# MoE ends by TensorE: first pair's rows picked, and last four experts' rows spread, by matrix products

## The reference, cut to what matters

```
t = rms_norm(h) (512 x 1024)
group = argmax of 4 group logits; p_group = its softmax value
the two best of the 8 experts in that group, weights softmax(top values) * p_group
y[token] = sum over its 2 experts of weight * (silu(t w1[e]) * (t w3[e])) w2[e]
h = h + y
```

## Time and profile before

| | us |
|---|---|
| median of 3 runs | 1840.77 (1838.44 to 1843.23) |
| the profiled execution | 1835.3 |
| its span, first to last instruction | 1833.6 |
| PE busy in it | 1609.1 |

### The profile page before, as it was taken

How to read it: one execution, slowest core, us unless ns; L and a number is a source line. 1 busy time by engine, 2 the same in 40 slices (tenths; PEclk the granted TensorE clock), 3 DMA queues, 4 the chain that set the end, 5 groups by cost and what they waited for, 6 DMA issues and landing times.

```text
span 1833.6 us, 26659 instructions
## 1 busy us (share of the span) xinstructions
PE 1609.1 (88%) x11565; PEld 840.2 (46%) x11565; DVE 600.6 (33%) x1162; ACT 416.6 (23%) x823; POOL 168.6 (9%) x189
## 2 busy tenths in 40 slices
PE   4999989998899999969878589999999997988871
PEld 2444468887454454534323244445544545333330
DVE  5210766663561121434111131206410324421114
ACT  2103245553300221301000120007511303010001
POOL 2000122330000000011111200000000000111102
PEclk9999999999899999979989879999999997998996
DMA  6119000000541411369999542211015024799994
GB/s 231 46 46 315 0 3 4 4 4 3 206 163 67 184 46 55 120 249 414 423 425 423 231 185 92 92 46 47 1 54 221 0 96 194 304 423 425 425 410 168
DMA packets 82071, 313.87 MB, mean 171 GB/s; under 512 B 18088, under 2 KB 19168, under 8 KB 57184
## 3 DMA queue, kind: packets, MB, share of 16 engines
q1 hardware_dynamic: 69280, 282.76, 39.3%
q0 software_dynamic: 11520, 25.19, 3.7%
q10 hardware_dynamic: 1152, 4.19, 0.6%
HBM read 305.81 MB, written 35.39 MB: 186 GB/s over the span
## 4 chain that ended last, share of the span: by engine, by line
PE 71%; issue 7%; DVE 5%; ACT 3%; DMA 2%; POOL 1%; PEld 0%; DVEq 0%; SPq 0%; POOLq 0%; ACTq 0%
PE PS L2097 14%; PE PS L545 14%; PE PS L559 11%; PE PS L1013 7%; PE PS L2122 6%; PE PS L1351 5%; PE PS L1337 2%; PE PS L2082 2%; PE PS L1313 1%; PE PS L1548 1%; PE PS L1569 1%; PE PS L484 1%; PE PS L1559 1%; PE PS L1701 1%; PE PS L1146 1%
## 5 line engine op out<-in xcount | busy, mean ns | idle before, releaser
L545 PE MATMUL PS<-arena,ring 128*128 128x512 f32 (+1 forms) x1024 | 414.9, 567 | 0.0
L545 PEld LDWEIGHTS PS<-arena,ring 128*128 128x128 f32 x1024 | 195.0, 191 | 216.4 <-issue 211.1
L559 PE MATMUL PS<-ring,arena 128*128 128x512 f32 x448 | 194.0, 592 | 0.7 <-ACT arena L1514 0.7
L2097 PE MATMUL PS<-ring,arena 128*64 128x512 f32 x512 | 131.6, 673 | 49.8 <-issue 46.8
L2097 PE MATMUL PS<-arena 128*64 128x512 f32 x512 | 121.8, 631 | 16.4 <-issue 13.6
L559 PEld LDWEIGHTS PS<-ring,arena 128*128 128x128 f32 x448 | 84.6, 190 | 104.3 <-issue 103.3
L1351 PE MATMUL PS<-ring,arena 128*128 128x512 f32 x256 | 113.6, 595 | 0.0
L2097 PEld LDWEIGHTS PS<-ring,arena 128*64 128x64 f32 x512 | 44.0, 155 | 135.5 <-issue 132.1
L2105 DVE TENSOR_TENSOR arena<-PS,arena 128x256 f32<-128x256 f32 x32 | 13.6, 425 | 273.8 <-PE PS L2112 253.4
L573 ACT ACTIVATE arena<-PS 128x512 f32<-128x512 f32 (+1 forms) x56 | 31.7, 566 | 307.4 <-PE PS L545 307.4
L2102 ACT ACTIVATE arena<-PS 128x256 f32<-128x256 f32 x32 | 12.3, 384 | 366.1 <-PE PS L2097 366.1
(11 more groups left out here) (295 smaller groups left out, 1923.8 us busy)
## 6 DMA issues: line engine op xcount, KB each, us to landing
arena<-in_moe_w SPq DMA_DIRECT2D x96, 1024.0 KB, 8.2
ring<-in_moe_w SPq DMA_DIRECT2D x96, 1024.0 KB
ring<-in_sb_wqkv SPq DMA_DIRECT2D x6, 2048.0 KB, 8.1
ring<-in_xa_wkv SPq DMA_DIRECT2D x4, 2048.0 KB, 15.6
ring<-in_xa_wq SPq DMA_DIRECT2D x4, 2048.0 KB, 8.5
ring<-in_xa_wo SPq DMA_DIRECT2D x4, 2048.0 KB, 13.7
h<-in_x SPq DMA_DIRECT2D x8, 512.0 KB, 5.2
ring<-in_rw_wr SPq DMA_DIRECT2D x2, 2048.0 KB, 13.2
```

Source lines behind the costliest of these rows:

```text
L545: ins = pe.matmul(PS[:, g % NBANK, 0:n], ring[:, u % RING, k, P * (j % 4):P * (j % 4) + P], xt[:, k, 0:n], start=(k == 0), stop=(k == KC - 1))
L559: ins = pe.matmul(PS[:, g % NBANK, :], xt[:, k, P * t:P * t + P], ring[:, (u0 + half) % RING, k, :], start=(k == 0), stop=(k == KC - 1))
L2097: ins = pe.matmul(bank(2, 2, F)[r, :, :], xgT[p][:, k, r], w[a][:, :, k, :], start=(k == 0), stop=(k == KC - 1))
```

## The change

It has three parts, in both layers.

1. The rows of the first pair are no longer gathered. `place` adds, for each tile, four DVE operations that make a matrix `first_of` (128 tokens x 128 slots) with 1/rms where a token stands in a slot of pair 0. In `moe_route_pe`, PE multiplies h by it (`first_rows`, 8 products of 128 x 128 x 128 for each of the 4 tiles, summed in banks 0 and 1), which gives the rows already turned. `first_rows(0)` stands ahead of `route_ranks(3)`, and `first_rows(1)` and `(2)` stand ahead of the last `filled_table`. POOL fetches from pair 1 on.
2. The outputs of pairs 14 and 15 (four experts) are no longer stored. They stay in the two buffers `ye`. While pairs 5 and 9 run, DVE makes their gate matrices (`spread_vec`, 12 operations each), PE turns them at pairs 7 and 11 (`spread_pe`, 4 transpositions each), DVE copies them out at 8 and 12 (`spread_out`). At the end PE multiplies them with `ye` (`combine_last_pe`, 4 tiles x 2 halves x 2 pairs = 16 products of 128 x 128 x 512), and DVE adds the result from PSUM to h (`combine_last_vec`, 8 additions of 128 x 512). ACT copies out both halves of pair 15.
3. The gathers of `moe_combine_pool` wait for the stores of pairs 0 to 13 alone and no longer for `over_done`; their additions (`combine_stored`) stand behind DVE's last copy of the pipeline. SP's loads for layer 1 no longer wait for the gathers. In `sb_proj_pe`, the turn of tile t waits for tile t + 1 too.

The weights are split over `w_stored`, `w_last` and `w_over` by 8 further small DVE operations in `over_slots` and `over_rows`. The block for experts with over 64 tokens uses other buffers and adds its rows by itself; that part of the diff, and lines of counts and addresses, are left out here.

```diff
@@ -1445,7 +1445,7 @@
 
         def sb_proj_pe(pe):
             for t in range(NT):
-                late_turn(pe, "mix1", t, lambda e, t: e.wait_ge(S("h_moe0"), t + 1))
+                late_turn(pe, "mix1", t, lambda e, t: e.wait_ge(S("h_moe0"), min(t + 2, NT)))
             project_T(pe, FIRST["sq"], UNITS.index("sqkv"), xTS, T, lambda e, k: late_there(e, "mix1", k))
             pe.wait_ge(S("mix1_diag"), NT)
             for t in range(NT):
...
@@ -1720,16 +1727,29 @@
 
         def moe_route_pe(pe, l):
             def filled_table(t):
-                pe.wait_ge(S("onehots"), 28 * l + 3 * (t + 1))
+                pe.wait_ge(S("onehots"), 32 * l + (5, 9, 12, 15)[t])
                 for k in range(2):
                     ins = pe.matmul(PS[:, 5, 0:NPE], OS[:, t, k, :], OB[:, t, k, :], start=(t + k == 0),
                                     stop=(t + k == NT))
                 return ins
 
+            def first_rows(t):
+                pe.wait_ge(S("onehots"), 32 * l + (5, 9, 12, 16)[t])
+                for k in range(KC):
+                    ins = pe.matmul(bank(k // 4, 4, P)[:, k % 4, :], h[:, t, k::KC], first_of[:, t, :],
+                                    start=(t == 0 and k % 4 == 0), stop=(t == NT - 1 and k % 4 == 3))
+                return ins
+
             for t in range(NT - 1):
                 filled_table(t)
+            first_rows(0)
             route_ranks(pe, l, NT - 1)
+            first_rows(1)
+            first_rows(2)
             filled_table(NT - 1).then_inc(S("tabled"), 1)
+            for p in range(2):
+                pe.nop().then_inc(S(f"xg_free{p}"), 1)
+            first_rows(NT - 1).then_inc(S("xg_free0"), 1)
             pe.wait_ge(S("chosen"), 2 * NT * (l + 1))
             scores_read(pe, l, 8)
             pe.matmul(PS[:, 4, 384:384 + NE], ones[:, :], cum[:, NT, :], start=True, stop=True).then_inc(S("ranked"), 1)
...
@@ -1846,6 +1866,15 @@
                     vec.tensor_scalar(OS[:, t, k, :], iob, s8[:, m:m + 1], tokid[:, t:t + 1], ALU.is_equal, ALU.mult)\
                         .then_inc(S("onehots"), 1)
 
+                w = first_w[:, :]
+                do(vec.tensor_scalar(w, OB[:, t, :, 0], rstd[:, t:t + 1], None, ALU.mult))
+                for k in range(2):
+                    m = NT * k + t
+                    ins = vec.tensor_scalar(first_k[:, k, :], iob, s8[:, m:m + 1], w[:, k:k + 1], ALU.is_equal, ALU.mult)
+                do(ins)
+                vec.tensor_tensor(first_of[:, t, :], first_k[:, 0, :], first_k[:, 1, :], ALU.add)\
+                    .then_inc(S("onehots"), 1)
+
             for t in range(NT):
                 add(0, t)
             vec.wait_ge(S("iota_ready"), 12)
...
@@ -1965,6 +1996,13 @@
             do(vec.tensor_tensor(den, den, gsum, ALU.mult))
             do(vec.reciprocal(wA, den))
             do(vec.tensor_tensor(wB, wA, ed, ALU.mult))
+            w8 = masks[:, 3, 28:36]
+            do(vec.tensor_tensor(w_over, w8, g8, ALU.mult))
+            do(vec.tensor_tensor(w_stored, w8, w_over, ALU.subtract))
+            do(vec.tensor_tensor(w_last[1], w_stored, is_15, ALU.mult))
+            do(vec.tensor_tensor(is_late, w_stored, is_late, ALU.mult))
+            do(vec.tensor_tensor(w_last[0], is_late, w_last[1], ALU.subtract))
+            do(vec.tensor_tensor(w_stored, w_stored, is_late, ALU.subtract))
             vec.wait_ge(S("tabled"), 9 * l + 9)
             vec.tensor_scalar(table[:, NPE:NCOL], PS[:, 5, NPE:NCOL], float(NO_ROW), None, ALU.add)\
                 .then_inc(S("over_known"), 1)
@@ -2041,11 +2079,11 @@
             pool.wait_ge(S("xg_cleared"), 2 * l + 2)
             pool.wait_ge(S("rows_out"), 16 * NT * (l + 1))
             pool.wait_ge(S("table_ready"), l + 1)
-            for n in range(4):
+            for n in range(1, 4):
                 fetch(n)
             pool.wait_ge(S("out_rows_known"), l + 1)
             pool.wait_ge(S("spare_filled"), 16 * (NE * BLK // T + 2))
-            for n in range(NPE):
+            for n in range(NPE - 2):
                 if n + 4 < NPE:
                     fetch(n + 4)
                 pool.wait_ge(S("ye_a"), NPE * l + n + l + 2)
@@ -2058,24 +2096,67 @@
         def moe_combine_pool(pool, l):
             pool.wait_ge(S("pos_known"), l + 1)
             for p in range(2):
-                pool.wait_ge(S(f"ye_out{p}"), 16 * (NPE // 2) * (l + 1))
-            pool.wait_ge(S("over_done"), l + 1)
+                pool.wait_ge(S(f"ye_out{p}"), 16 * stored(p) * (l + 1))
             for t in range(NT):
                 for k in range(2):
                     pool.indirect_dma_start(out=yg[2 * t + k], out_offset=None, in_=scratch["blocks"],
                                             in_offset=bass.IndirectOffsetOnAxis(ap=pos[:, t, k:k + 1], axis=0))\
                         .then_inc(S(f"yg_in{t}"), 16)
 
-        def moe_combine_vec(vec, l):
+        def combine_stored(vec, l, t):
+
+
+            vec.wait_ge(S(f"yg_in{t}"), 32 * (l + 1))
+            for k in range(2):
+                m = NT * k + t
+                vec.scalar_tensor_tensor(out=h[:, t, :], in0=yg[2 * t + k], scalar=w_stored[:, m:m + 1], in1=h[:, t, :],
+                                         op0=ALU.mult, op1=ALU.add).then_inc(S("h_stored"), 1)
+                vec.wait_ge(S("h_stored"), 8 * l + 2 * t + k + 1)
+
+        def last_bank(t, half):
+
+            return (4 + 2 * t + half) % 8
+
+        def combine_last_pe(pe, l):
+            pe.wait_ge(S("gates_last"), 10 * l + 6)
+            pe.wait_ge(S("ye_a"), (NPE + 1) * (l + 1))
+            pe.wait_ge(S("ye_v"), (NPE + 1) * (l + 1))
             for t in range(NT):
-                vec.wait_ge(S(f"yg_in{t}"), 32 * (l + 1))
-                for k, w in enumerate((wA, wB)):
-                    if k:
-                        vec.wait_ge(S("h_half"), NT * l + t + 1)
-                    vec.scalar_tensor_tensor(out=h[:, t, :], in0=yg[2 * t + k], scalar=w[:, t:t + 1], in1=h[:, t, :],
-                                             op0=ALU.mult, op1=ALU.add)\
-                        .then_inc(S("h_half") if k == 0 else S(f"h_moe{l}"), 1)
-
+                for half in range(2):
+                    for p in range(2):
+                        ins = pe.matmul(PS[:, last_bank(t, half), :], gatesT[p][:, t, :],
+                                        ye[p][:, 512 * half:512 * half + 512], start=(p == 0), stop=(p == 1))
+                ins.then_inc(S("gates_last"), 1)
+
+        def combine_last_vec(vec, l):
+            for t in range(NT):
+                vec.wait_ge(S("gates_last"), 10 * l + 7 + t)
+                for half in range(2):
+                    v = h[:, t, 512 * half:512 * half + 512]
+                    ins = vec.tensor_tensor(v, v, PS[:, last_bank(t, half), :], ALU.add)
+                ins.then_inc(S(f"h_moe{l}"), 1)
+
+        def spread_vec(vec, l, p):
+
+
+            do = stepper(vec, l)
+            for t in range(NT):
+                for k in range(2):
+                    m = NT * k + t
+                    do(vec.tensor_scalar(gates_k[:, k, :], iob, s8[:, m:m + 1], w_last[p][:, m:m + 1], ALU.is_equal,
+                                         ALU.mult))
+                do(vec.tensor_tensor(gates_n[:, t, :], gates_k[:, 0, :], gates_k[:, 1, :], ALU.add))
+            vec.nop().then_inc(S("gates_last"), 1)
+
+        def spread_pe(pe, l, p):
+            pe.wait_ge(S("gates_last"), 10 * l + 3 * p + 1)
+            for t in range(NT):
+                ins = pe.transpose(PS[:, 3, P * t:P * t + P], gates_n[:, t, :], ident[:, :])
+            ins.then_inc(S("gates_last"), 1)
+
+        def spread_out(vec, l, p):
+            vec.wait_ge(S("gates_last"), 10 * l + 3 * p + 2)
+            vec.tensor_copy(gatesT[p].rearrange("p t s -> p (t s)"), PS[:, 3, :]).then_inc(S("gates_last"), 1)
 
         def turn_rows(pe, p, rows):
             for k in range(KC):
...
@@ -2162,14 +2248,12 @@
                 pe.wait_ge(S("ye_v"), NPE * l + n + l + 1)
                 down(pe, p, 2, 1).then_inc(S("down_done"), 1)
 
-            pe.wait_ge(S("table_ready"), l + 1)
-            for p in range(2):
-                pe.nop().then_inc(S(f"xg_free{p}"), 1)
-            turn(0)
             for n in range(NPE):
                 up_pair(n)
                 if n == 4:
                     over_table_pe(pe, l)
+                if n in (7, 11):
+                    spread_pe(pe, l, n // 11)
                 if n:
                     turn_hid_of(n - 1)
                 if n + 1 < NPE:
@@ -2188,6 +2272,11 @@
                 ye_free(act, l, n // 2, p)
                 d, s = ye_half(p, P, 0)
                 act.activation(d, s, ACT.Copy).then_inc(S("ye_a"), 1)
+                if n == NPE - 1:
+                    act.wait_ge(S("down_done"), NPE * l + n + 1)
+                    d, s = ye_half(p, P, 1)
+                    act.activation(d, s, ACT.Copy).then_inc(S("ye_v"), 1)
+
             act.wait_ge(S("table_ready"), l + 1)
```

(75 more changed lines are left out.)

6 lines of the change are left out of this document (3 added, 3 removed).

## The result

| | before | after |
|---|---|---|
| median | 1841.11 us (1838.44 to 1843.23, 5 runs) | 1832.01 us (1828.32 to 1833.91, 5 runs) |
| ratio | | 0.9942, 95% interval 0.9929 to 0.9955 |
| the profiled execution | 1835.3 | 1833.91 |
| its span | 1833.6 | 1832.2 |

The change brought 9.1 us where 22.6 were forecast. The result stands 13.8 us above the predicted 1818.2 and 2.0 above the top of the range.

The account below looks back on a forecast made before the run. The MoE's middle was taken to wait for weights (DMA saturated), with exposed chains at its start and end. Front 7.9 plus back 7.3 and 7.4 make 22.6 us: 1840.8 to 1818.2 us, range 1808 to 1830.

Parts of the forecast that it names:

- the price of a record of `first_rows`: Products replacing pair 0's fetch: 0.107 us a record at full clock, doubled at the lower, from L1452.
- The bound: Price limits for first_rows of one tile, 16 records: 1.7 us at full clock or 3.4 at the lower.
- The first `up` at the full clock: First big product of each MoE: clock rises during first_rows(2), so this up takes 7.09 us.
- rival B: Clock rises early, with first_rows(0): front gains 17.3 us, sum 32.0, time 1808.8; chance 0.15.
- Rival C: Clock does not rise before the first up: front -3.2 us, sum 11.5, time 1829.3; chance 0.13.
- a gain in front is passed on: Middle of the MoE: an earlier first up starts the DMA-saturated stretch earlier and moves its end by as much.
- Rival E: Front gains nothing because the loads are held elsewhere: sum 14.7 us, time 1826.1; chance 0.07.
- The back: MoE end, last four experts by products without stores, branch and gathers in the chain: gains 7.4 and 7.3 us.
- Product pass: MoE end: 16 products of 128 x 512, 32 records, take 13.7 us at the full clock.
- pair 13's store: Issued at 1780.9, gathers following from about 1785 and landed by 1801, so DVE is not late.
- Rival D: Product pass at the end runs at 1.2 GHz, 27.5 us for 13.7: time 1845.7 or 1856.8; chance 0.05.
- the front: MoE start, pair 0's fetch removed: first up ends 4.9 and 3.0 us earlier in the two layers, 7.9 in all.

Follow-up runs that it names:

- e3: Changed kernel, but first_rows reads 128 neighbouring features as stationary operand, so pair 0's result is not right: 1822.92 us, ratio 0.9874 to the kernel before.
- e6: Changed kernel with first_rows' operands exchanged: first_of stationary, h moving 512 columns, rows copied and then turned by PE: 1820.71 us, ratio 0.9869 to the kernel before.
- e7: Changed kernel, but ACT writes normed rows in turned order and first_rows and turn_rows read neighbours: 1816.89 us, ratio 0.9850 to the kernel before.
- e4: Changed kernel with PE's branch over the full-experts block moved behind the product pass: 1831.10 us, ratio 0.9940 to the kernel before.
- e5: The changed kernel run again, nothing edited: 1833.02 us, ratio 0.9951 to the kernel before.
- e2: The kernel before with first_rows alone, nothing of the back: 1847.39 us, ratio 1.0029 to the kernel before.
- e1: Changed kernel with first_rows taken out, pair 0's fetch and turn back, so the back alone: 1828.72 us, ratio 0.9926 to the kernel before.

## Why the prediction was wrong

**The step that failed is the price of a record of `first_rows`.** The forecast took L1452 as "the nearest" row and 0.107 us a record at the full clock, double at the lower. Measured: 0.25 at the lower, 0.24 at the full. L1452's stationary operand is 128 neighbours; `h[:, t, k::KC]` takes every eighth float. The form of a row, 128 x 128, does not tell this; the code does. From the start of `first_rows(1)`, 15.8 us after L1351 (15.6 forecast), (1) and (2) took 1.9 us too long and (3) 2.2, with the table and the copies 0.5: `up` started 29.6 us after L1351, not 25.0. e3 changes the spread alone and has the forecast's times; e6 and e7, which avoid it in other ways, have them too. That settles this cause.

The bound was wrong with it. "No row has exactly this product" is true of the product, but not of its operand: the kernel before turns rows by transpositions whose stationary operand has the same stride of 8 floats (L2082, L484), beside others that read 128 neighbours (L1559). Asked by themselves in the kernel before:

```profile
L2082 PEld LDWEIGHTS PS<-ident,arena x256: 186/189/230, 796.0 to 1775.4; 128*128 128x128 f32 x128
L1559 PEld LDWEIGHTS PS<-ident,arena x160: 137/140/143, 1242.7 to 1310.5; 128*128 128x128 f32 x160
```

The spread load is the longer one, 189 ns against 140. It didn't slow the turns, as 8 of them take 1.04 us at the full clock (818.77), so these rows warn of the load and don't give the pace of a stream of products. The price of `first_rows` should have had an upper end far above L1452's, at the full clock as well. The Trainium skill, page "SBUF — State Buffer", section "Door 1: The DMA port swizzle", says that reading at full rate needs two hits in each 16-byte line, so that 4 floats of stride are free. Here the stride is 8 floats, and it isn't free at the full clock: 336 ns against 192. No run here tests a stride of 4 floats.

**The first `up` at the full clock** was the second miss, 1.7 us a layer. The clock rose during `first_rows`, 4.2 us after `first_rows(1)` had begun in layer 0, where 4.8 were forecast. That nearness is in part luck: over the 14 layers of the profiles with `first_rows` the rise came from 14.4 to 21.1 us after L1351, and in four of them (one each in e4, e5, e6 and e7) before `first_rows(1)` had begun. None rose at the start of `first_rows(0)`, as rival B has it; the earliest came 3.1 us behind it. That the clock would stay up was taken for granted. In the four profiles with the spread operand (the changed kernel twice, e2, e4) the first `up` took 8.8 to 10.0 us in 7 of 8 layers; in e3, e6 and e7 it took 7.1 in 6 of 6. The gap ahead of the `up` is no difference: PE stands idle 1.71 us in front of it in e3 as in the changed kernel. Together the misses make 6.3 us in layer 0, and the `up`'s end lies 6.4 and 6.2 us behind the forecast (38.5 against 32.1, 39.1 against 32.9). Rival C came near by its number (1829.3), but not by its reason: the clock did rise.

**That a gain in front is passed on** held in every run. From the end of the first `up` to the start of the last one it was 211.7 to 212.7 us in both layers of all 9 profiles, wherever the first `up` ended. Rival E is out: in e3 the earlier `up` came through.

**The back** was right in its parts. Product pass: 13.99 us for 32 records (13.7). Its start: 1.37 us after the last `down` record in 8 of 14 cases, some 0.8 us after that record's end (0.95). From the last `down`, e1, e3, e4 and e5 have 24.0 to 24.5 and 29.2 to 29.5, so 8.2 to 8.7 and 7.0 to 7.3 gained (7.4 and 7.3). By medians e1 has 12.9 of 14.7. One length beside the path was off: pair 13's store, taken to land in some 4 us, took 8.0 to 8.9 from its issue in e1, e3 and e4. DVE had slack for that in layer 0 of e1, e3, e4 and e5, and none in e6 and e7.

Rival D did not come; a smaller form did, in one layer: the pass at 1802.89 began at the lower clock and took 15.4 us.

**The sum by what was measured:** back -12.9 (e1), front +5.8 (e2): -7.1, by the medians -9.1. Forecast: -14.7 and -7.9, together -22.6. Of the 15.5 us between -7.1 and -22.6, the front makes 13.7 and the back 1.8.

**Left open.** The late handover of the changed kernel's profile, 2.48 and 3.43 us from the last `down` record to the pass and not 1.37. It was there in both layers of that profile, in layer 1 of e6 (2.40) and, smaller, in both of e7 (1.65 and 2.09) and in layer 1 of e5 (1.53), when the same kernel ran again; layer 0 of e5 had 1.37. The gathers keep DMA at a share near 1 at that time in all of these, and in punctual ones too. The runs show that the branch is not needed for either outcome; what delays it they don't show. Why the clock falls again after a pass with the spread operand, and what sets the moment of its rise, is open as well. No kernel was run with other gaps or loads there.

## What to carry to other kernels

Take a matrix product's price from a row whose stationary operand has the same stride, not only the same shape; if there is none, let the range hold a price that doesn't shrink with the clock. Ask for the duration of the load (PEld) as well as for the pace of the records: a longer load can be hidden in one use and set the pace in another. When a fetch is replaced by TensorE work in front of a saturated stretch, every microsecond until the first big product's end counts one for one, so run each half of a change alone before keeping both. And after a gain, look for what was just hidden: here a store beside weight loads, for which POOL waits 8.7 us, and the gathers behind it were next.

## What the runs showed of the hardware that was not expected

- A load of a 128 x 128 float32 stationary operand with a stride of 8 floats took 336 ns at both levels of the clock, a contiguous one 333 at the lower and 192 at the full one. A record of the product then came every 0.24 us at the full clock, and not 0.12.
- `first_rows` began at 790.3 in e3 and at 790.1 in the changed kernel, with PE and PEld busy 1.00 in both up to the rise; the clock rose near 795.5 in one and near 798.9 in the other. The operand alone does not set this: in e5, the changed kernel again, it rose 15.1 us after L1351 in layer 0 and 21.1 in layer 1.
- An indirect store beside saturated weight loads took 8.0 to 8.9 us from issue to landing (pair 13's in e1, e3 and e4); before, with no load beside it, 2.87.
- A transposition's load of 128 x 128 with the stride of 8 floats took 189 ns (L2082, before), one of neighbours 140 (L1559), at the same pace of the records (0.11 us at the full clock in both).
- ACT's copy of 128 x 1024 float32 took 2.14 us when it read with a stride of 8 floats (e7), and 1.14 when it read neighbours (the changed kernel).
